# The level products of a pair of heads issued alternately, in a decoder block on one Trainium2 core

## The reference, cut to what matters

```python
bc = jnp.cumsum(to_chunks(gk), axis=3)
...
diff = bi[:, :, :, None, :] - bi[:, :, None, :, :]
decay = jnp.exp(jnp.where(mask, diff, -jnp.inf))
attn = jnp.einsum('bhid,bhjd,bhijd->bhij', qi, ki, decay)
o = jnp.einsum('bhij,bhjv->bhiv', attn, vi) + \
    jnp.einsum('bhid,bhdv->bhiv', qi * jnp.exp(bi), S)
```

## Time and profile before

| | |
|---|---|
| median of 3 runs | 1272.07 us (1272.0 to 1273.05) |
| span of the profiled execution | 1274.5 us |
| mean granted TensorE clock in it | 0.975 |
| TensorE busy | 1241.6 us, 97% of the span |
| VectorE, ScalarE, POOL busy | 43%, 25%, 24% |
| records on line 1181 (level products) | 384 loads, 384 matmuls, first at 105.7 us, last at 223.2 us |

### The profile page before, as it was taken

The page is one execution under the profiler, slowest core; times in us unless marked ns, Lnnn a source line. Parts: engine busy times, 40 slices in busy tenths (PEclk is TensorE's granted clock), DMA queues, the critical chain, the costliest instruction groups (busy, mean ns, idle before and its releaser), DMA issues.

```text
span 1274.5 us, 14329 instructions
## 1 busy us (share of the span) xinstructions
PE 1241.6 (97%) x5856; PEld 1032.0 (81%) x5856; DVE 552.8 (43%) x727; ACT 319.4 (25%) x419; POOL 309.4 (24%) x114
## 2 busy tenths in 40 slices
PE   6999999999999999999999999999999999999994
PEld 5788899977788888888888888888888888887883
DVE  6456547642744432333232333333333324395345
ACT  7321111214432311111121212121211212174332
POOL 2111214512321221212121121203030404172203
PEclk9898888899999999999999999999999999999997
DMA  6210101101310411110102020202020201001003
GB/s 219 83 33 33 34 1 34 34 33 66 133 47 21 165 50 50 35 64 33 66 13 86 3 96 0 99 0 99 0 99 0 99 0 74 0 1 63 29 1 132
DMA packets 15125, 67.75 MB, mean 53 GB/s; under 512 B 1889, under 2 KB 2802, under 8 KB 8818
## 3 DMA queue, kind: packets, MB, share of 16 engines
q1 hardware_dynamic: 15090, 67.26, 14.7%
HBM read 63.06 MB, written 4.19 MB: 53 GB/s over the span
## 4 chain that ended last, share of the span: by engine, by line
PE 92%; DVE 5%; ACT 1%; DMA 1%; issue 0%; SPq 0%; DVEq 0%
PE pb L1067 28%; PE pb L1068 28%; PE pb L1069 28%; PE pb L1181 3%; DVE e_lo L687 1%; PE pb L1169 1%; PE pb L1168 1%; DVE h L996 1%; PE pb L1103 1%; DMA w_raw<-in_w_in_dram 1%; PE pb L1147 1%; DVE sums L697 1%; PE pb L1162 1%; DVE sums L669 0%; PE pb L1096 0%; DVE mix_lo L901 0%
## 5 line engine op out<-in xcount | busy, mean ns | idle before, releaser
L369 POOL TENSOR_TENSOR w_lo<-w_raw,w_hi 128x2048 fp32r<-128x2048 f32 (+2 forms) x53 | 231.5, 4375 | 864.6 <-ACT w_hi L457 864.6
L1067 PE MATMUL pb<-f_hi,w_hi 128*128 128x512 f32 x704 | 274.7, 390 | 0.0
L1068 PE MATMUL pb<-f_lo,w_hi 128*128 128x512 f32 x704 | 274.2, 389 | 0.0
L1069 PE MATMUL pb<-f_hi,w_lo 128*128 128x512 f32 x704 | 274.1, 389 | 0.0
L996 DVE TENSOR_TENSOR h<-h,pb 128x512 f32<-128x512 f32 x176 | 119.8, 686 | 87.5 <-PE pb L1069 87.4
L1067 PEld LDWEIGHTS pb<-f_hi,w_hi 128*128 128x128 f32 x704 | 132.2, 188 | 27.6 <-issue 0.2
L1068 PEld LDWEIGHTS pb<-f_lo,w_hi 128*128 128x128 f32 x704 | 132.2, 188 | 27.5 <-issue 0.2
L1069 PEld LDWEIGHTS pb<-f_hi,w_lo 128*128 128x128 f32 x704 | 132.2, 188 | 27.4
L1067 PE MATMUL pb<-gu_hi,w_hi 128*128 128x512 f32 x352 | 137.2, 390 | 0.0
L1068 PE MATMUL pb<-gu_lo,w_hi 128*128 128x512 f32 x352 | 137.1, 389 | 0.0
L1069 PE MATMUL pb<-gu_hi,w_lo 128*128 128x512 f32 x352 | 137.1, 389 | 0.0
(11 more groups left out here) (149 smaller groups left out, 1703.5 us busy)
## 6 DMA issues: line engine op xcount, KB each, us to landing
w_raw<-in_w_ffn_gate_dram SPq DMA_DIRECT2D x11, 1024.0 KB, 4.7
w_raw<-in_w_ffn_up_dram SPq DMA_DIRECT2D x11, 1024.0 KB, 4.8
w_raw<-in_w_ffn_down_dram SPq DMA_DIRECT2D x11, 1024.0 KB, 4.7
w_raw<-in_w_in_dram SPq DMA_DIRECT2D x8, 1024.0 KB, 4.9
h<-in_x_t_dram SPq DMA_DIRECT2D x16, 256.0 KB, 6.9
w_raw<-in_w_out_dram SPq DMA_DIRECT2D x4, 1024.0 KB, 5.8
h<-in_x_t_dram SPq DMA_DIRECT2D x8, 512.0 KB, 5.1
w_raw<-in_w_ple_gate_dram SPq DMA_DIRECT2D x4, 1024.0 KB, 4.8
```

Of the source, the lines that this page charges most:

```text
L369: nc.gpsimd.tensor_tensor(w_lo[s][:, 0:size], w_raw[s][:, 0:size], w_hi[s][:, 0:size].bitcast(F32), ALU.subtract).then_inc(w_lo_ready[s], 1)
L1067: M(bank, w_h, x_h, start=start, stop=False)
L1068: M(bank, w_h, x_l, start=False, stop=False)
L1069: return M(bank, w_l, x_h, start=False, stop=stop)
```

## The change

The two fills of a group become one function, `level_fills`. It claims both banks first, then issues the eight products of the two heads in turn: head 0, head 1, head 0, and so on, each head into its own bank as before. The last product of each head raises `aux.filled`. Operands, banks, masks, drains, and the place of the group among the units are as before.

```diff
-                elif kind == "o" or kind in range(NEAR) and n:
+                elif kind == "o":
                     pass
...
-                elif n == 0:
-                    pe.wait_ge(scaled_ready, 2 * (kind + 1))
...
-                else:
-                    s = LEVELS[kind]
-                    sc = scaled[:, kind % 2, :].rearrange("p (a t c) -> p a t c", a=KP, c=C)
-                    for j in range(4 * KP):
-                        t, a = 4 * c + j // KP, j % KP
+                i.then_inc(aux.filled, 1)
+
+            def level_fills(lev, c):
+                s, f = LEVELS[lev], FILL[lev, 2 * c]
+                if c == 0:
+                    pe.wait_ge(scaled_ready, 2 * (lev + 1))
+                aux.claim(f + 1)
+                sc = scaled[:, lev % 2, :].rearrange("p (a t c) -> p a t c", a=KP, c=C)
+                for j in range(4 * KP):
+                    t, a = 4 * c + j // KP, j % KP
+                    for r in range(2):
+                        rows = slice(r * DK, (r + 1) * DK)
                         right = sc[rows, a, t, :].rearrange("p (n s) -> p n s", s=2 * s)[:, :, s:2 * s]
-                        i = M(bank[:, j * C // 2:(j + 1) * C // 2], sc[rows, a, t, :], right, start=True, stop=True)
-                i.then_inc(aux.filled, 1)
+                        i = M(aux.bank(f + r)[:, j * C // 2:(j + 1) * C // 2], sc[rows, a, t, :], right, start=True, stop=True)
+                        if j == 4 * KP - 1:
+                            i.then_inc(aux.filled, 1)
 
             def fills_after(b, j):
                 for kind, n in FILLS_AFTER.get((b, j), []):
-                    fill(kind, n)
+                    if kind not in range(NEAR):
+                        fill(kind, n)
+                    elif n % 2 == 0:
+                        level_fills(kind, n // 2)
```

## The result

The changed kernel takes 1245.53 us (median of 4 executions, 1243.76 to 1247.46), the kernel before 1272.56 us (median of 4). The ratio is 0.978, with a 95% interval of 0.9763 to 0.9796: 2.2% faster. Forecast were 1242 us and a range of 1238 to 1256. The profiled execution spans 1245.5 us, 29.0 less than the one before.

A forecast was written before the change was run, and what follows sets the result against it. TensorE's own stream was taken as the bound. Shorter level groups (18.4 us) and a steady clock behind them (12.5) sum to 30.9 us off the 1274.5 us span, 1243.6, median 1241.2, forecast 1242; range 1238 to 1256.

The forecast's parts named there:

- The group: Level products: both heads side by side take 1.90 us a group; twelve groups save 18.4 us.
- the kv group: Kv products alternating between column halves, 32 records in 1.90 us; taken as model for level group time and steady clock.
- The clock behind the groups: Projection units after level groups: no clock drop left behind the shorter groups, 12.5 us less, bounds 0 and 12.5.
- the six long stretches: Group end to next group start, 7.11 to 8.58 us at six places; claimed to fall to 5.68 and 5.94 us.
- The margin of 0.6 us at block 6: Block 6's low halves come at 15.1 us, needed at 15.7: no wait, but almost.
- the prediction's own sign: Last listed check, at block 6: the prediction is wrong there if TensorE waits for POOL.
- The last step of the sum: Whole kernel: median of the runs taken as 2.4 us below the profiled span, turning 1243.6 into 1241.2 us.
- the drop after the near products: Clock drop at 232 us: may come or not at its new place, 3 us either way.
- The half overlap: Level products: only one load per product slips under the other head, groups 2.77 us, 1265.5 us; chance 0.10.
- the side-by-side start: Change of head inside a group: overlap comes only from the semaphore between fills, so nothing gained; chance 0.02.
- The slower rival: Level products: each change of head empties the array, adding 33.6 us, 1306 us; chance 0.03.
- The feeders: Ahead of block 6's low halves: VectorE slowed beside POOL, TensorE waits 3.7 us, about 1246 us; chance 0.07.

The follow-up runs named there:

- the experiments on the order: Changed kernel, both banks still claimed first, but eight products of head 0 issued before the eight of head 1: 1273.76 us, ratio 1.000.
- a single row half: Changed kernel, products alternating between the two banks but all sixteen reading partitions 0 to 63: 1292.2 us, ratio 1.0123.
- the kv products: Changed kernel with kv products issued one half of the columns after the other instead of alternately: 1245.61 us, ratio 0.9769.
- the later ones: Changed kernel unaltered, measured once more beside the kernel before: 1244.79 us against 1274.13 us, ratio 0.9777.
- two by two: Changed kernel with the heads changing after every two level products instead of every one: 1241.99 us, ratio 0.9744.
- four by four: Changed kernel with the heads changing after every four level products: 1250.85 us, one execution.
- the output products: Changed kernel with output products of two heads taken together, 64-row products alternately first, then the 128-row ones: 1238.61 us, ratio 0.9718.
- the squares first: Changed kernel with output products in pairs, and ScalarE squaring the last four output fills before making the high halves: 1237.53 us, ratio 0.9704.

## Why the prediction was right

*The group.* Forecast 1.90 us, measured 1.93. That the two row halves run side by side was read from two rows, the four loads in flight at the change of head and the kv group; the experiments on the order, on a single row half and on the kv products show both readings to be true. Only the reach was read one short: TensorE finds the other head's work behind three records, not two. The twelfth group of before, which the sum of 41.15 us counts, is this one:

```profile
220.13 3.32 PE pb L1181 x32
```

Together the groups save 41.15 - 12 x 1.93 = 18.0 us, less the wait at block 6, where 18.4 were forecast.

*The clock behind the groups.* Forecast 12.5 us, by analogy with the kv group, and measured close to that: five of the six long stretches are 5.67 to 5.95 us now, the sixth, across the start of block 6, about 6.2 with the wait there. This was the weakest step, since six equal groups had no drop behind them; the experiments that doubled and halved the groups are what shows it, not the result.

*The wait that comes next.* The margin of 0.6 us at block 6 turned into a wait of 0.23 us. The low halves came 16.0 us after unit (5, 2) began (176.87 less 160.86) where 15.1 were reckoned: POOL's instruction took 5.61 us instead of 4.62, with an instruction of VectorE beside it that kept its 1.23 us, where before it was VectorE's that took long (5.49 us); the rest of the chain was as reckoned. The wait was named and placed rightly, with a price close to nothing; by the prediction's own sign, no wait for POOL at block 6, this step was wrong by these 0.23 us.

*From the span to the median.* 30.9 us forecast, 30.2 measured in the stage, 29.0 in the span, 27.0 between the medians of the first runs, 29.3 between those of the later ones. The stage came within 0.7 us of the sum. The rest is sampling: where the clock falls differs between executions of either kernel, and one execution of each was profiled. The last step of the sum, which took the median to lie 2.4 us below the span, compared two different executions: in each execution with both figures the time is about 2 us above its own span (1247.46 us beside a span of 1245.5). The profiled execution of before was thus one of its slow ones, near 1276.5 us by estimate, and the median of the changed kernel came out 3 us above the 1242 of the forecast. I named the drop after the near products as the open one; the one that came was at 1119.71 us, just behind a short wait of TensorE (1.84 us for the sums of a norm) that the kernel before has as well (1.77 us), without a drop. The second profile of the changed kernel has the wait and no drop either, so it is nothing that the change brings about every time; what decides it is open.

*The rivals.* The half overlap does not hold in these traces: matmuls begin at twice the pace of one stream, and two by two has groups of 1.98 us. But the prediction priced it wrongly. Starts in program order, each half keeping its own step of 0.109 us, let every second record start with the one before it, so the changed kernel's order would need 17 steps, about 2.0 us by estimate, not 2.77. The changed kernel's 1.93 us alone would hardly have told the two apart; two by two does, with 25 steps, 2.9 us by the same estimate, against 1.98, and four by four with 29, 3.3 us, against 2.54. The rule of the Trainium skill ("TensorE: Matmul & The Clock Gate", Part 3, The mechanism) that matmuls start strictly in program order does not agree with these traces. By its order of starts a group would take these 17 steps, and not the 2.77 us that the prediction put to it. The ends of matmuls are modelled, so they say nothing of its other half, the order of the ends. That the side-by-side start came only from the semaphore between the two fills is ruled out by groups of 1.93 us that have none between the heads. The slower rival, an array that empties at each change of head, is ruled out by the same groups. The feeders did not become the bound in this stage, but did with the output products, by the mechanism that this rival named: VectorE beside POOL, 9.03 us for four instructions that took 2.50 with the squares first.

## What to carry to other kernels

Small float32 products that use only half of the array's rows or columns cost little more than half as much here when two independent streams on different halves are issued alternately (1.93 us where one stream took 3.71); every one or two products will do, every four leaves 0.6 us of the 1.4 us that a group gained. The row halves went to two banks in all these runs; one bank was not tried. Look for a place in the trace where two such streams already meet: here one change of head was enough to foresee the effect. And count what the clock does behind thin work as part of its price: here it was two fifths of the gain (12.5 us of 30.9 in the sum).

## What the runs showed of the hardware that was not expected

- TensorE starts work of the other half of the array some three records (load and matmul each) ahead of its turn, matmuls included: 2.9 to 3.4 steps hidden at each change, by rows and by columns alike (groups of 3.32 and 2.54 us with 1 and 3 changes; kv 2.50 us with 3). With 7 changes both streams run throughout (1.98 us).
- Sixteen products on one row half in two banks keep a step of 0.11 us: two banks alone bring no overlap, and the kv products overlap by column halves within one bank.
- At two streams for 3.72 us the clock stayed at full twelve times of twelve; at one stream for 3.71 us or more it fell twelve times of twelve, and at one stream for 3.32 us or more six times of twelve in one trace, nine in another.
- Beside POOL's low halves VectorE needed 9.03 us for four instructions that took 2.50 without them.
